# Gate and up products of a decoder block on one NeuronCore: two matmuls that share their weights joined into one of 512 columns

## The reference

```
h2 = rmsnorm(x, norm_ffn)
g = causal_dwconv(h2 @ ffn_w_gate, ffn_conv_w)            # 2048 x 5632, 3 taps along the tokens
x = x + (silu(g) * (h2 @ ffn_w_up)) @ ffn_w_down          # 2048 x 5632, then 5632 x 2048
```

## Time and the profile before

| | us |
|---|---|
| median of 3 runs | 2180.36 (2176.31 to 2181.01) |
| the profiled execution | 2179.13 |
| its span | 2177.3 |
| TensorE busy, matmuls | 2148.2 (99%) |
| VectorE busy | 1430.9 (66%) |
| GpSimd busy | 1296.5 (60%) |
| ScalarE busy | 982.1 (45%) |
| DMA, mean rate | 145 GB/s |

### The profile page before, as it was taken

The page is one execution under the profiler, slowest core; times in us unless marked ns, Lnnn a source line. Parts: engine busy times, 40 slices in busy tenths (PEclk is TensorE's granted clock), DMA queues, the critical chain, the costliest instruction groups (busy, mean ns, idle before and its releaser), DMA issues.

```text
span 2177.3 us, 40359 instructions
## 1 busy us (share of the span) xinstructions
PE 2148.2 (99%) x14948; PEld 1976.2 (91%) x14948; DVE 1430.9 (66%) x2266; ACT 982.1 (45%) x1386; POOL 1296.5 (60%) x730
## 2 busy tenths in 40 slices
PE   8999999999999999999999999999999899999999
PEld 6777777887888888999999999999999899999999
DVE  6489565677763226777777777777777656566566
ACT  6343344343334445454454454454454444444444
POOL 5345334454545565767767667677677566666665
PEclk9999999999999999999999999999999999999999
DMA  5324223333334443444543544444444875566544
GB/s 198 84 76 123 64 68 93 106 98 97 102 97 133 146 136 130 158 137 135 173 140 135 169 140 145 159 146 150 156 140 162 304 267 198 179 207 211 186 130 135
DMA packets 153615, 316.26 MB, mean 145 GB/s; under 512 B 13177, under 2 KB 57913, under 8 KB 153497
## 3 DMA queue, kind: packets, MB, share of 16 engines
q1 hardware_dynamic: 103552, 252.23, 35.7%
q10 hardware_dynamic: 49944, 62.45, 8.9%
HBM read 265.31 MB, written 49.18 MB: 144 GB/s over the span
## 4 chain that ended last, share of the span: by engine, by line
PE 87%; DVE 8%; DMA 2%; issue 2%; ACT 1%; SPq 0%; POOL 0%; ACTq 0%; DVEq 0%
PE ps L841 20%; PE ps L842 20%; PE ps L843 20%; PE ps L652 9%; PE ps L654 8%; PE ps L653 8%; DVE work L1375 1%; DMA raw<-w_dn 1%; DVE work L1374 1%; DVE work L1278 1%; PE ps L748 0%; PE ps L734 0%; DVE sqsum L1511 0%; DVE work L1277 0%; DVE work L1305 0%
## 5 line engine op out<-in xcount | busy, mean ns | idle before, releaser
L841 PE MATMUL ps<-comb,fhi 128*128 128x256 f32 x3584 | 1017.7, 284 | 13.0 <-POOL flo L608 6.9
L842 PE MATMUL ps<-comb,flo 128*128 128x256 f32 x3584 | 1016.8, 284 | 0.0
L843 PE MATMUL ps<-comb,fhi 128*128 128x256 f32 x3584 | 1016.7, 284 | 0.0
L608 POOL TENSOR_TENSOR flo<-raw,fhi 128x1024 fp32r<-128x1024 f32 (+2 forms) x252 | 487.2, 1934 | 379.9 <-ACT fhi L1149 374.6
L841 PEld LDWEIGHTS ps<-comb,fhi 128*128 128x128 f32 x3584 | 690.7, 193 | 14.4 <-POOL flo L608 7.3
L842 PEld LDWEIGHTS ps<-comb,flo 128*128 128x128 f32 x3584 | 690.6, 193 | 0.3 <-issue 0.2
L843 PEld LDWEIGHTS ps<-comb,fhi 128*128 128x128 f32 x3584 | 690.7, 193 | 0.0
L578 POOL TENSOR_TENSOR wlo<-raw,whi 128x512 fp32r<-128x512 f32 x260 | 375.5, 1457 | 392.6 <-ACT whi L948 341.9
L608 POOL TENSOR_TENSOR flo<-sum,fhi 128x1024 fp32r<-128x1024 f32 (+2 forms) x168 | 324.1, 1930 | 68.2 <-ACT fhi L1149 66.9
L652 PE MATMUL ps<-hhi,whi 128*128 128x512 f32 x784 | 318.6, 406 | 3.8 <-DVE hlo L1515 3.8
L1149 ACT ACTIVATE fhi<-ps 128x1024 fp32r<-128x1024 f32 (+2 forms) x168 | 141.4, 842 | 392.2 <-DVE ps L1592 277.4
(11 more groups left out here) (211 smaller groups left out, 2504.6 us busy)
## 6 DMA issues: line engine op xcount, KB each, us to landing
raw<-w_gu SPq DMA_DIRECT2D x176, 512.0 KB, 3.5
raw<-w_in SPq DMA_DIRECT2D x196, 256.0 KB, 3.1
raw<-w_dn SPq DMA_DIRECT2D x96, 256.0 KB, 3.0
raw<-w_dn SPq DMA_DIRECT2D x64, 320.0 KB, 3.1
act_hi<-thi ACTq DMA_DIRECT2D x22, 896.0 KB, 4.9
act_lo<-tlo ACTq DMA_DIRECT2D x22, 896.0 KB, 9.4
raw<-w_out SPq DMA_DIRECT2D x64, 256.0 KB, 3.2
comb<-act_hi SPq DMA_DIRECT2D x28, 512.0 KB, 4.0
```

Source lines behind the costliest of these rows:

```text
L608: nc.gpsimd.tensor_tensor(flo[s][:, 0:w], src[:, 0:w], fhi[s][:, 0:w].bitcast(F32), ALU.subtract).then_inc(f_lo_pool, 1)
L841: nc.tensor.matmul(dst, fhi[s][:, w], high, start=fresh and k == 0, stop=False, skip_group_check=True)
L842: nc.tensor.matmul(dst, flo[s][:, w], high, start=False, stop=False, skip_group_check=True)
L843: ins = nc.tensor.matmul(dst, fhi[s][:, w], low, start=False, stop=k == n - 1, skip_group_check=True)
```

## The change

- **Matmuls of gate and up.** In each block, the products of the high weights with the high and with the low activations become one matmul of 512 columns (`both`), whose result fills the whole bank: the high-high part in columns 0 to 255, the high-low part in columns 256 to 511 (`small`). The low-high matmul of 256 columns stays, and goes first.
- **Readouts.** The two halves of a bank are added as VectorE reads them: one more operation at each place. p1v gets its second half on VectorE (`p1_full`), and the next X product waits for that; X at the fourth product goes through a copy by ScalarE (`p12v`) and a sum. New semaphores count these steps.
- **S3 = A11-A21** is made by GpSimd (`make_s3`) from raw11 and raw21, between the last `low_unit` of a unit (pos 6) and that of the next unit's first factor (pos 0), in the gate and up units and in the down units. `sum2` no longer waits for it. SyncE's load of A21 now does, in place of the load of A11.
- **The first tap** goes to ScalarE (`first_tap`), behind the copy p1v.
- **`activate`** moves on VectorE from behind `sum1` to behind the readout of the late gate.

```diff
@@ SyncE, unit(u)
                 sp_.wait_ge(copied21, lin(u, 1, 0))
+                sp_.wait_ge(sum3_ready, lin(u, 1, 0))
                 weights(u, A21, raw21, loaded21)
...
                 sp_.wait_ge(sum2_ready, lin(u, 1, 0))
-                sp_.wait_ge(sum3_ready, lin(u, 1, 0))
                 weights(u, A11, raw11, loaded11)
@@ GpSimd
+            def make_s3(u):
+
+                w = width(u)
+                pool.wait_ge(loaded21, lin(u, 16, 16))
+                pool.wait_ge(loaded11, lin(u, 16, 16))
+                if u == 0:
+                    pool.wait_ge(w_used, QN_END - 2)
+                else:
+                    pool.wait_ge(f_hi, lin(u, 7, -2))
+                    pool.wait_ge(f_lo_pool, lin(u, 5, -2))
+                nc.gpsimd.tensor_tensor(sum3[:, 0:w], raw11[:, 0:w], raw21[:, 0:w], ALU.subtract).then_inc(sum3_ready, 1)
...
                 low_unit(n, 6, raw22[lane(n) % 2])
                 if n != NUNIT - 1:
+                    make_s3(step(n, 1))
                     low_unit(step(n, 1), 0, raw11)
@@ TensorE, product()
+                    if gate_up(u):
+
+                        both = block_of(b)[:, :, k, :]
+                        nc.tensor.matmul(dst[:, 0:HT], flo[s][:, w], both[:, HI, :], start=fresh and k == 0, stop=False, skip_group_check=True)
+                        ins = nc.tensor.matmul(dst, fhi[s][:, w], both, start=False, stop=k == n - 1, skip_group_check=True)
+                        continue
@@ ScalarE
+            def first_tap(j):
+
+                weight = pc[:, bass.ds(lin(j, 3, PC["fcw"] + 2), 1)] if not isinstance(j, int) else par("fcw", 3 * j + 2)
+                sc.wait_ge(x_read, lin(j, 1, 1))
+                sc.wait_ge(z_read, lin(j, 2, 2))
+                sc.wait_ge(up_early, lin(j, 1, 1))
+                A(bank(MLP), gpad[:, 2:], ACT.Copy, scale=weight).then_inc(tap0_done, 1)
...
+                if gate_up(n):
+
+                    sc.wait_ge(f_used, lin(n, 7, 4))
+                    if n != 0:
+                        sc.wait_ge(mlp_step, lin(n, 6, -3))
+                    A(p12v[:, :], stream(X), ACT.Copy).then_inc(p12_copied, 1)
                 if more:
                     high_p1(step(n, 1))
@@ VectorE, gate_up_unit(n)
                 sum4_(n)
-                if not first:
-                    tap(step(n, -1), 0)
+                ve.wait_ge(f_used, lin(n, 7, 1))
+                ve.wait_ge(p1_copied, lin(n, 1, 1))
+                V.tensor_tensor(p1v[:, :], small(X), p1v[:, :], ALU.add).then_inc(p1_full, 1)
...
                 sum1(step(n, 1))
-                if not first:
-                    activate(step(n, -1))
...
                 ve.wait_ge(f_used, lin(n, 7, 4))
-                V.tensor_tensor(gpad[:, 2 + HT:2 + T], stream(X), sqsum[:, late], ALU.mult).then_inc(x_read, 1)
-                sum3_(step(n, 1))
+                ve.wait_ge(p12_copied, lin(n, 1, 1))
+                V.tensor_tensor(small(X), small(X), p12v[:, :], ALU.add).then_inc(mlp_step, 1)
+                if not first:
+                    ve.wait_ge(taps_done, lin(n, 2, 0))
+                ve.wait_ge(mlp_step, lin(n, 6, 3))
+                V.tensor_tensor(gpad[:, 2 + HT:2 + T], small(X), sqsum[:, late], ALU.mult).then_inc(x_read, 1)
+                if not first:
+                    activate(step(n, -1))
                 if pair:
                     act_sums(n, 0)
...
-                V.tensor_tensor(stream(MLP), stream(Y), p15v[:, :], ALU.add).then_inc(y_read, 1)
+                V.tensor_tensor(upv[:, early], stream(Y), p15v[:, :], ALU.add).then_inc(up_part, 1)
+                ve.wait_ge(up_part, lin(n, 2, 1))
+                V.tensor_tensor(stream(MLP), small(Y), upv[:, early], ALU.add).then_inc(y_read, 1)
```

More of the change, by code:

```diff
@@ L430, in stream, with small @@
             return bank(t)[:, 0:HT]
+        def small(t):
+            return bank(t)[:, HT:T]
         LEFT, RIGHT = 2, 4
@@ L631, in _ @@
             low_unit(0, 0, raw11)
+            make_s3(0)
             low_h2(KT - 1)
@@ L851, in gate_up_unit @@
                     pe.wait_ge(x_read, lin(n, 1, 0))
-                product(n, 0, stream(X), True, (lambda k: pe.wait_ge(h2_lo_even, k + 1)) if first else None)
+                product(n, 0, bank(X), True, (lambda k: pe.wait_ge(h2_lo_even, k + 1)) if first else None)
                 pe.wait_ge(f_lo_dve, lin(n, 2, 1))
@@ L856, in gate_up_unit @@
                     pe.wait_ge(z_read, lin(n, 2, 0))
-                product(n, 1, stream(Z), True)
+                product(n, 1, bank(Z), True)
                 pe.wait_ge(f_lo_dve, lin(n, 2, 2))
@@ L864, in gate_up_unit @@
                     pe.wait_ge(y_read, lin(n, 3, 0))
-                product(n, 2, stream(Y), True)
+                product(n, 2, bank(Y), True)
                 if first:
@@ L1613, in up_late @@
                 ve.wait_ge(f_used, lin(j, 7, 7))
-                V.tensor_tensor(stream(Y), stream(Y), p1v[:, :], ALU.add).then_inc(up_sum, 1)
-                ve.wait_ge(up_sum, lin(j, 1, 1))
-                V.tensor_tensor(upv[:, late], stream(Y), sqsum[:, late], ALU.mult).then_inc(y_read, 1)
+                ve.wait_ge(p1_full, lin(j, 1, 1))
+                V.tensor_tensor(upv[:, late], stream(Y), p1v[:, :], ALU.add).then_inc(up_part, 1)
+                ve.wait_ge(up_part, lin(j, 2, 2))
+                V.tensor_tensor(small(Y), small(Y), upv[:, late], ALU.add).then_inc(mlp_step, 1)
+                ve.wait_ge(mlp_step, lin(j, 6, 6))
+                V.tensor_tensor(upv[:, late], small(Y), sqsum[:, late], ALU.mult).then_inc(y_read, 1)
             def tap(j, i):
                 weight = pc[:, bass.ds(lin(j, 3, PC["fcw"] + 2 - i), 1)] if not isinstance(j, int) else par("fcw", 3 * j + 2 - i)
[L1621 to L1625, removed]
-                else:
-                    ve.wait_ge(taps_done, lin(j, 3, i))
-                    V.scalar_tensor_tensor(bank(MLP), gpad[:, 2 - i:2 - i + T], weight, bank(MLP), ALU.mult, ALU.add).then_inc(taps_done, 1)
+                if i == 1:
+                    ve.wait_ge(tap0_done, lin(j, 1, 1))
+                else:
+                    ve.wait_ge(taps_done, lin(j, 2, 1))
+                V.scalar_tensor_tensor(bank(MLP), gpad[:, 2 - i:2 - i + T], weight, bank(MLP), ALU.mult, ALU.add).then_inc(taps_done, 1)
             def activate(j):
@@ L1664, in gate_up_unit @@
                 sum4_(n)
-                if not first:
-                    tap(step(n, -1), 0)
+                ve.wait_ge(f_used, lin(n, 7, 1))
+                ve.wait_ge(p1_copied, lin(n, 1, 1))
+                V.tensor_tensor(p1v[:, :], small(X), p1v[:, :], ALU.add).then_inc(p1_full, 1)
                 ve.wait_ge(f_used, lin(n, 7, 2))
-                ve.wait_ge(p1_copied, lin(n, 1, 1))
-                V.tensor_tensor(p15v[:, :], stream(Z), p1v[:, :], ALU.add).then_inc(z_read, 1)
+                ve.wait_ge(p1_full, lin(n, 1, 1))
+                V.tensor_tensor(p15v[:, :], stream(Z), p1v[:, :], ALU.add).then_inc(mlp_step, 1)
+                ve.wait_ge(mlp_step, lin(n, 6, 1))
+                V.tensor_tensor(p15v[:, :], small(Z), p15v[:, :], ALU.add).then_inc(z_read, 1)
                 if not first:
@@ L1675, in gate_up_unit @@
                 ve.wait_ge(f_used, lin(n, 7, 3))
-                V.tensor_tensor(p16v[:, :], stream(Y), p1v[:, :], ALU.add).then_inc(y_read, 1)
+                V.tensor_tensor(p16v[:, :], stream(Y), p1v[:, :], ALU.add).then_inc(mlp_step, 1)
+                ve.wait_ge(mlp_step, lin(n, 6, 2))
+                V.tensor_tensor(p16v[:, :], small(Y), p16v[:, :], ALU.add).then_inc(y_read, 1)
                 sum1(step(n, 1))
-                if not first:
-                    activate(step(n, -1))
                 if first:
@@ L1704, in gate_up_unit @@
                 ve.wait_ge(f_used, lin(n, 7, 6))
-                V.tensor_tensor(stream(Z), stream(Z), p16v[:, :], ALU.add).then_inc(gate_sum, 1)
-                ve.wait_ge(gate_sum, lin(n, 1, 1))
-                V.tensor_tensor(gpad[:, 2:2 + HT], stream(Z), sqsum[:, early], ALU.mult).then_inc(z_read, 1)
+                V.tensor_tensor(p16v[:, :], stream(Z), p16v[:, :], ALU.add).then_inc(mlp_step, 1)
+                ve.wait_ge(mlp_step, lin(n, 6, 4))
+                V.tensor_tensor(small(Z), small(Z), p16v[:, :], ALU.add).then_inc(mlp_step, 1)
+                ve.wait_ge(mlp_step, lin(n, 6, 5))
+                V.tensor_tensor(gpad[:, 2:2 + HT], small(Z), sqsum[:, early], ALU.mult).then_inc(z_read, 1)
                 sum2(step(n, 1))
@@ L1774, in _ @@
             sum1(0)
-            sum3_(0)
             low_s1(0)
```

41 lines of the change are left out of this document (16 added, 25 removed).

## The result

The changed kernel takes 2199.18 us (median of 4 runs, 2192.7 to 2199.43), the kernel before 2179.45 us beside it (4 runs, 2176.31 to 2181.01): ratio 1.0085, 95% interval 1.0063 to 1.0107. It is slower by 0.85%, against a forecast of 2201 us. The profiled execution was the shortest, 2192.7 us; two more taken later were 2192.95 and 2194.41 us.

What follows compares the result with a forecast made beforehand. TensorE was taken to bound gate and up by matmul count times spacing. 2179.1-33.5 (matmuls)+42 (stall)+10 (clock)+2 (down stage) = 2199.6, and the runs' median 1.2 above the profiled one gives 2201 us; range 2150 to 2226.

Steps and rivals of the forecast that it cites:

- The sign and its mechanism: Gate and up: slower, as a 2.0 us stall ahead of the seventh product in 21 even units outweighs 33.5 us saved.
- The matmuls: Gate and up: 0.3464 in place of 0.360 us at each of 2464 places, saving 33.5 us.
- The stall: Even units, seventh product waiting for VectorE's up sum: 2.0 us late in 21 units, +42 us.
- The order of the two: `act_sums` part 0: first subtraction waits for `make_s3`'s end, the second for GpSimd's whole next low part.
- My own test: Even units: the forecast is wrong if the second subtraction records 0.41 us; the time then falls to 2150.
- The clock: TensorE behind the stalls: falls to 1.2 GHz, 0 to 31 us, a third taken, +10 us.
- Costs set at nothing: Gate and up: VectorE's extra readouts (+3.0 us per unit) covered by the products; ScalarE's p12v and first tap hidden.
- The down stage: Down stage: no gain from moving `sum3_`; a few A21 loads come late, +2 us, from 0 to 8.
- The second subtraction not held: Rival, even units: second subtraction not held behind a whole GpSimd operation, stall 0.06 to 0.3 us; 2150 or 2155; chance 0.24.
- The stall that just cancels the gain: Rival, even units: earliest `make_s3`, stall 1.6 us, no fall of the clock; 2183 us; chance 0.10.
- The joined matmul costing two: Rival, gate and up: the joined matmul costs two, products stay 2.88 us, stall 1.8 us; 2225 us; chance 0.04.

Runs made afterwards that it cites:

- Sums later: Changed kernel with `act_sums` part 0 moved behind `low_s1` and parts 1 and 2 behind `sum2`; 2148.88 us, ratio 0.989 to the kernel before.
- S3 behind the next low part: Changed kernel with `make_s3` behind the low part of the next unit's first factor instead of ahead of it; 2211.75 us, ratio 1.015 to the kernel before.
- sums later, without the join: Changed kernel with the `act_sums` sums moved later and three matmuls of 256 columns again; 2177.44 us, ratio 1.0003 to the kernel before.
- S3 of eight columns: Changed kernel with GpSimd's S3 sum covering only 8 columns behind the first unit; 2160.98 us, ratio 0.9927 to the kernel before.
- the three kernels without pauses: Sums later alone, with the wide matmul first, and with the first tap back on VectorE; 2148.88, 2147.25 and 2145.42 us.
- the unjoined form: Changed kernel with the joined matmul split again, three matmuls of 256 columns; 2205.91 us, ratio 1.0134 to the kernel before.

## Why the prediction came out right

**The sign and its mechanism held.** The gain of the matmuls was there, and VectorE's two subtractions in part 0 of `act_sums`, held by GpSimd's back-to-back operations, made the seventh product late in every even unit from 2 on, and in no odd one. The measured 2199.2 us stands 1.8 below the forecast. "Sums later" takes this one cause away and gives the gain back.

**The matmuls.** Joined and narrow take 0.3467 us as the sum of the earlier trace rows had it, 32.8 us for the stage. That the two runs of the moving operand cost nothing held as well. What no row before showed is the second level, 0.3533.

**The stall.** Term by term from the fourth product seen: `make_s3` at 1.08 (forecast 1.15), the first subtraction wanted at 2.02 (1.86), up sum at 6.38 (6.30), the matmul at 7.31 (7.33), due at 5.28 (5.34). So 2.03 us in that unit for a forecast of 2.0. Over all 21 units the mean is 1.80, with 0.11 for the slower first block behind a restart, which I had not counted: 40.0 us for the forecast 42.

**The order of the two was wrong in most units.** The step said that "the engines alternate, and the second subtraction pays a whole GpSimd operation". In 12 of 21 units it was the first that paid for both, and the second recorded 0.41 us. My own test, "I am wrong if the second subtraction records 0.41 us in even units: then the time falls to 2150", would have misled: it came true in these units, and the time didn't fall, since the sum of the two is what counts. In the three profiles of the changed kernel the kinds part by when the first asks: 0.94 to 1.07 us behind the start of `make_s3` it was held for both (28 units), 1.12 to 1.37 behind it was let in at the end (35). That is no rule by itself. In "S3 behind the next low part" the first asked 0.60 to 0.67 us behind the start of a low part, earlier than any of these, and was let in at its end in all 21 units. So what decides between the two stays open. Of the 21 units, the seven that follow a stretch at 0.3533 us are all of the second kind: their fourth product comes some 0.3 us later against GpSimd. Their pause is 0.6 us shorter, and that pays back most of the 0.75 us that the slower blocks cost a pair of units; therefore 7, 10 or 14 such stretches move the changed kernel's time by little.

**The clock** was the term that was mis-sized for the profiled executions. I took 10 us, a third of all stalls. None of the 21 pauses was followed by 1.2 GHz in the first profile, none in the second, and one in the third (the restart at 1214.66, starts 2.36 apart; 1.5 us). In "S3 behind the next low part" it was 5 of 21 with pauses 0.1 to 0.2 us longer. So the size of a fall, 1.5 to 1.6 us, held, and its chance at this length was too high. In the profiled execution other parts made up for much of it: -10 for the clock, -2 for the stall, -1.5 for the down stage, -1.2 in unit 0, against +5.2 for the slower blocks, +0.7 for the matmuls and +1.9 ahead of the stage, -6.9 in all. The sum's 2199.6 less that is 2192.7, the time of the execution.

That the median nevertheless sits at 2199.2 is not shown by a profile. Its three longer runs (2199.07, 2199.43 and 2199.29 us) have mean granted clocks of 0.993, 0.995 and 0.995, the profiled one 0.996. A mean lower by 0.001 to 0.003 means that another 0.2 to 0.6% of the span passed at half speed, so 2 to 7 us, an estimate; and the slow blocks could carry little. But the executions of the kernel before have mean clocks of 0.995 to 0.998 as well, within 6 us. So some of the clock term may be in the median, but the agreement of the forecast to 0.1% is partly luck.

**Costs set at nothing.** Seven more readouts, p12v and the tap: "sums later, without the join" equals the kernel before to 0.03% with all of them in. **The down stage** took 0.5 us more from its first block to the end, for a forecast of 2; ScalarE's copy of A21 waited for its load twice there, 6.4 us in all; in the kernel before it was once, also 6.4 us.

**The rivals.** The second subtraction not held (2150) is what "sums later" made real, 2148.9. The stall that just cancels the gain (2183) needed 1.6 us; the second kind of pause has 1.45, so it is that rival's case, but in a third of the units only. The joined matmul costing two (2225) is refuted by the spacing.

The Trainium skill, "TensorE: Matmul & The Clock Gate", section "Back-to-back issue gap", gives 2.5 ns on top of the columns for an isolated matmul. Taken over to this stream, as the prediction did, it would have the join worth 6 us, an estimate from that page; "sums later" against its unjoined form has 28.6, so the measurement decides. The Trainium skill, "GPSIMD Engine Reference", section "Specifications", names the contention of GpSimd with VectorE's instructions of two SBUF inputs; the trace agrees, with 0.41 us free and up to 4.11 us held.

**What stays open.** What sets a level of 0.3467 or 0.3533 us at a restart; what makes the changed kernel's executions of 2199 us; which pauses of 2.3 to 2.6 us are followed by 1.2 GHz; and when a held subtraction is let in behind the first GpSimd operation, and when only behind the second.

## What to carry to other kernels

Before work is added to GpSimd, look on VectorE for instructions with two SBUF inputs that stand ahead of a readout: their price can be the rest of what GpSimd does without a gap (here of two operations; longer rows were not tried), not their own 0.4 us, and one place further on in the queue it is nothing. Count that price as the sum over neighbouring instructions, since which of them records it depends on tenths of a microsecond. And when a bound engine's stretches get shorter, work out the slack of every reader again: without the join the same waits cost 28 us, with it 40.

## What the runs showed of the hardware that I had not expected

- **Two levels of a matmul stream.** The same alternating matmuls of 256 and 512 columns run at 0.3467 or 0.3533 us a block, at a granted clock of 1.00 in both. With no stop of TensorE one level held for some 830 us; with stops it changed, even at restarts of 0.1 us (S3 of eight columns), where a few changes also came without a visible stop. Three matmuls of 256 columns were at 0.360 us in every profiled execution. Of the 16 executions of the three kernels without pauses, four are some 16 us longer than the rest; the one of them that was profiled had the slower level throughout.
- **A held VectorE instruction can be passed over.** With two GpSimd operations of 2.4 us end to end it waited for both, 4.1 us, in 28 units of the changed kernel's three profiles. In the other 35, and in all 21 with the two in the other order, it waited for the first only.
- **The first block after a pause** takes 0.42 to 0.46 in place of 0.347 us at full clock. Behind the 1.25 us pauses of the unjoined form it is 0.43 to 0.46 in place of 0.360.
